# One attention stage for latent and grouped attention, one-hot expert rows, early preparation of the second block

## The reference

```python
p = h @ w_in
cq, ckv, kr = p[..., :o0], p[..., o0:o1], p[..., o1:o2]
gq, gk, gv = p[..., o2:o3], p[..., o3:o4], p[..., o4:]
qa = (rmsnorm(cq, q_norm) @ w_q_up)    # latent attention
kva = (rmsnorm(ckv, kv_norm) @ w_kv_up)
qb = rmsnorm(gq per head, gq_norm)     # grouped attention, 2 key heads
x = x + g1 * (concat(oa, ob) @ w_out)
```

## Time and profile before

| | us |
|---|---|
| median of 3 runs (lowest, highest) | 3480.21 (3478.96, 3483.86) |
| profiled execution, its time | 3482.5 |
| profiled execution, its span | 3480.7 |
| first block ends, second block's first projection starts | 1564.1, 1607.6 |
| layer 0's output projection starts | 1928.05 |
| layer 0's experts start, layer 1's | 2036.9, 2938.3 |

### The profile page before, as it was taken

The page is one execution under the profiler, slowest core; times in us unless marked ns, Lnnn a source line. Parts: engine busy times, 40 slices in busy tenths (PEclk is TensorE's granted clock), DMA queues, the critical chain, the costliest instruction groups (busy, mean ns, idle before and its releaser), DMA issues. The chain is left out here.

```text
span 3480.7 us, 31524 instructions
## 1 busy us (share of the span) xinstructions
PE 2873.4 (83%) x12630; PEld 1621.3 (47%) x12630; DVE 1009.5 (29%) x2513; ACT 571.0 (16%) x1269; POOL 239.2 (7%) x408
## 2 busy tenths in 40 slices
PE   6799989998799999995788868788838986877874
PEld 3476646854476547843456432232214463322221
DVE  2443423413443514402155321111123153111112
ACT  1222401101223301102223110000000141000000
POOL 0000004000000000000000000110011020011001
PEclk9999999999999999997898879899968987989997
DMA  5245445534155434533300359999974213999996
GB/s 205 74 162 207 146 145 170 194 136 145 50 192 202 150 139 162 177 115 73 109 25 25 117 211 427 428 427 427 426 305 118 73 43 125 428 427 427 428 427 243
DMA packets 188683, 740.54 MB, mean 213 GB/s; under 512 B 16400, under 2 KB 25600, under 8 KB 163440
## 3 DMA queue, kind: packets, MB, share of 16 engines
q1 hardware_dynamic: 163600, 667.51, 49.1%
q0 software_dynamic: 24928, 70.90, 6.2%
HBM read 711.52 MB, written 28.67 MB: 213 GB/s over the span
## 5 line engine op out<-in xcount | busy, mean ns | idle before, releaser
L2063 PE MATMUL bank<-wslot,xgT 128*64 128x512 f32 x1040 | 541.0, 681 | 187.5 <-DMA wslot<-in_moe_w_up 94.1
L2064 PE MATMUL bank<-wslot,xgT 128*64 128x512 f32 x1040 | 542.3, 682 | 0.0
L458 PE MATMUL bank<-h1T,wslot 128*128 128x256 f32 x2176 | 482.8, 385 | 3.0 <-DVE fpad L1464 3.0
L458 PEld LDWEIGHTS bank<-h1T,wslot 128*128 128x128 f32 x2176 | 417.8, 193 | 62.9 <-issue 6.5
L2063 PEld LDWEIGHTS bank<-wslot,xgT 128*64 128x64 f32 x1040 | 156.5, 156 | 512.1 <-issue 512.1
L2080 DVE TENSOR_TENSOR hid<-gs,bank 64x512 f32<-64x512 f32 x65 | 67.9, 1045 | 696.9 <-ACT gs L2074 696.9
L2118 PE MATMUL bank<-wslot,aT 128*64 128x512 f32 x1040 | 230.6, 595 | 2.8 <-DVE aT L532 1.5
L435 PE MATMUL bank<-wslot,hT 128*128 128x512 f32 (+3 forms) x576 | 224.7, 553 | 5.1 <-issue 4.3
L435 PEld LDWEIGHTS bank<-wslot,hT 128*128 128x128 f32 x576 | 113.3, 198 | 111.9 <-issue 99.3
L2064 PEld LDWEIGHTS bank<-wslot,xgT 128*64 128x64 f32 x1040 | 156.5, 156 | 8.7 <-issue 8.7
L435 PE MATMUL bank<-wslot,actT 128*128 128x512 f32 x352 | 151.5, 593 | 5.6 <-DVE actT L1503 5.6
(11 more groups left out here) (342 smaller groups left out, 3196.3 us busy)
## 6 DMA issues: line engine op xcount, KB each, us to landing
wslot<-in_moe_w_gate SPq DMA_DIRECT2D x65, 2048.0 KB, 17.2
wslot<-in_moe_w_up SPq DMA_DIRECT2D x65, 2048.0 KB, 12.8
wslot<-in_moe_w_down SPq DMA_DIRECT2D x65, 2048.0 KB, 15.8
wslot<-in_w_in SPq DMA_DIRECT2D x36, 2048.0 KB, 9.0
wslot<-in_w_ada SPq DMA_DIRECT2D x24, 2048.0 KB, 8.1
wslot<-in_ffn_w_up SPq DMA_DIRECT2D x20, 2048.0 KB, 8.7
y_rows<-yo POOLq DMA_DIRECT2D x130, 128.0 KB, 7.1
wslot<-in_w_proj_ssd SPq DMA_DIRECT2D x8, 2048.0 KB, 7.8
```

Source lines behind the costliest of these rows:

```text
L458: ins = pe.matmul(b.t[:, 0:width], w[:, k, j * P:(j + 1) * P], xT(k), start=(k == 0), stop=(k == kc - 1))
L2063: pe.matmul(bk.t[other, :], xt.t[:, k, mine], wg[:, k, :], start=(k == 0), stop=(k == KD - 1))
L2064: ins = pe.matmul(bk.t[mine, :], xt.t[:, k, mine], wu[:, k, :], start=(k == 0), stop=(k == KD - 1))
```

## The change

- `joint_attention` takes the place of both attention functions. Its four projections from `hT` come first (`cq`, `ckv`, `gq`, `gkv`), then `qup` and `kvup`, all by `tokens_later`, and the plan's order follows. Then one pipeline of 64 jobs runs, context tiles first. Grouped queries are kept two heads to a tile (`qbT`), and the keys (`kbT`) are kept twice with the other half blanked, where before the queries were. `kaT` lies in `hT`'s memory.
- `Second` holds the second block's tensors from the start of the kernel. Its `beside` puts the modulation columns and the norms and transposes of the context tiles into `K.rest` during `first_ffn` of layer 1. Its `begin` scales and norms the latent tiles, and `ready(t)` writes a tile into `hT` just ahead of its `cq` matmuls.
- The gate row is fetched during the projections (`fetch_gate`), in both layers. `noted` records marks where `settle` stood after the attentions. `add_gated` waits tile by tile.
- Expert rows: `route` writes the normed rows into `hT`'s memory (`h_rows`) and stores nothing to `h_dram`. `select` builds for each pair a matrix of 0 and 1 per token tile on VectorE, and `turn_rows` multiplies the rows by it: 8 x 4 matmuls a pair in layer 0, 8 x 2 in layer 1. `gather`, `tokidx` and the steps that made it are gone.
- The first block's `acc`, `gate` and two `decay` buffers lie in the second block's tensors.

The diff, cut to its core:

```diff
...
+    def noted(self):
+
+        self.settled = [(s, s.count) for s in (self.pe, self.dve, self.act) if s.count]
...
+    def tokens_later(self, key, xT, n_tiles, deps, use, each=None):
...
+            ready = each(t) if each else ()
             bank = self.banks.next()
 
             @self.block.tensor
             def _(pe):
-                for due in self.due(pe, landed, *deps, *bank.free):
+                for due in self.due(pe, landed, *deps, *ready, *bank.free):
...
+        K.tokens_later(("cq",), xT, NT2, [], use_low(QL, "q_norm", cqT), hready)
+        K.tokens_later(("ckv",), xT, NT2, [], use_low(KVL, "kv_norm", ckvT), hready)
+        K.tokens_later(("gq",), xT, NT2, [], use_gq, hready)
+        K.tokens_later(("gkv",), xT, NT2, [], use_gkv, hready)
+        fetch_gate((K.pe, K.pe.count))
...
+            def use_q(t, bank, mk, n=n):
                 b = tok.next()
...
+            K.tokens_later(("qup", n), lambda k, t: cqT[:, k, t * P:(t + 1) * P], NT2, low, use_q)
...
+            K.tokens_later(("kvup", n), lambda k, t: ckvT[:, k, t * P:(t + 1) * P], NT2, low, use_kv)
+        projected = (K.pe, K.pe.count)
...
+        grouped_jobs(0)
+        grouped_jobs(1)
+        latent_jobs(0)
+        latent_jobs(1)
+        for t in range(2, NT2):
+            grouped_jobs(t)
+            latent_jobs(t)
         pipeline(jobs, 7)
-        K.settle()
...
+    def select(i):
         if i >= len(pairs):
             return
-        x, q = xg.next(), pairs[i][0] // 2
-
-        @block.gpsimd
-        def _(g):
-            sig = K.moved.next()
-            for due in K.due(g, (sig, sig.count) if sig.count else None, *routed, *x.free):
-                g.wait_ge(*due)
-            got[i] = (x, sig.mark(g.indirect_dma_start(
-                x.t[:, :], None, h_dram, bass.IndirectOffsetOnAxis(ap=tokidx[:, q:q + 1], axis=0)).then_inc(sig.sem, 16), 16))
+        a, f, s, q = away.next(), first.next(), sel.next(), pairs[i][0] // 2
+
+        @block.vector
+        def _(v):
+            for due in K.due(v, *slotted, *s.free):
+                v.wait_ge(*due)
+            m = K.dve.mark(v.tensor_scalar(a.t[:, :], slot[:, :], float(-PAIR * q), None, ALU.add).then_inc(K.dve.sem, 1))
+            for due in K.due(v, m):
+                v.wait_ge(*due)
+            for t in range(tiles):
+                m = K.dve.mark(v.tensor_scalar(f.t[:, t, :], K.c("iota"), a.t[:, 2 * t:2 * t + 1], None, ALU.is_equal)
+                               .then_inc(K.dve.sem, 1))
+            for due in K.due(v, m):
+                v.wait_ge(*due)
+            for t in range(tiles):
+                K.mv = K.dve.mark(v.scalar_tensor_tensor(out=s.t[:, t, :], in0=K.c("iota"), scalar=a.t[:, 2 * t + 1:2 * t + 2],
+                                                         in1=f.t[:, t, :], op0=ALU.is_equal, op1=ALU.add)
+                                  .then_inc(K.dve.sem, 1))
+        got[i] = (s, K.mv)
 
     def turn_rows(i):
...
-                    ins = pe.transpose(bk.t[:, j * P + pr.start:j * P + pr.stop], x.t[pr, kk * P:(kk + 1) * P],
-                                       K.ident[pr, pr])
+                    for t in range(tiles):
+                        ins = pe.matmul(bk.t[:, j * P:(j + 1) * P], h_rows[t][:, kk * P:(kk + 1) * P], s.t[:, t, :],
+                                        start=(t == 0), stop=(t == tiles - 1))
...
-    gather(0)
-    gather(1)
+    select(0)
     turn_rows(0)
+    select(1)
     for i in range(len(pairs)):
-        gather(i + 2)
         if i:
             turn_hidden(i - 1)
         widen(i)
         turn_rows(i + 1)
+        select(i + 2)
...
+        self.h_rows = [flat[:, D * t:D * (t + 1)] for t in range(self.tiles)]
...
-            step(v.tensor_scalar(qsu[:, 0, :], self.yrow[:, :], 7, None, ALU.logical_shift_right))
-            step(v.tensor_scalar(qsu[:, 1, :], self.yrow[:, :], PAIR - 1, None, ALU.bitwise_and))
-            step(v.tensor_copy(qsf[:, :, :], qsu[:, :, :]))
-            step(v.tensor_tensor(spot[:, :, :], bc(iota(PAIR).unsqueeze(1), TK, PAIR), bc(qsf[:, 1, :].unsqueeze(2), TK, PAIR),
-                                 ALU.is_equal))
-            step(v.tensor_tensor(pair[:, :, :], bc(iota(npair).unsqueeze(1), TK, npair),
-                                 bc(qsf[:, 0, :].unsqueeze(2), TK, npair), ALU.is_equal))
-            K.mv = step(v.tensor_tensor(ident[:, :, :, :], pair[:, :, :].rearrange("p (t k) n -> p t k n", k=2),
-                                        bc(K.c("token")[:, 0:T].unsqueeze(2).unsqueeze(2), T, 2, npair), ALU.mult))
-        placed = K.mv
-        b2 = K.banks.next()
-
-        @K.block.tensor
-        def _(pe):
-            for due in K.due(pe, placed, *b2.free):
-                pe.wait_ge(*due)
-            for i in range(TK):
-                ins = pe.matmul(b2.t[:, 0:npair], spot[:, i, :], ident[:, i // 2, i % 2, :], start=(i == 0), stop=(i == TK - 1))
-            K.mp = K.pe.mark(ins.then_inc(K.pe.sem, 1))
+            K.mt = step(v.tensor_copy(self.slot[:, :], self.yrow[:, :]))
         late, dif, ex, den = F("late", [T, 4]), F("dif", [T]), F("ex", [T, 4]), F("den", [T])
...
+        quiet = lambda: None
+        K.rest += [quiet, lambda: modulated(0), lambda: modulated(1), lambda: norm(0), lambda: norm(1), quiet, quiet,
+                   lambda: turn(0), quiet, lambda: turn(1)]
...
+            st, inv, m = K.inverse_rms((w["junk"], w["stat"]), x[:, t, :], D, *K.settled)
+
+            @K.block.vector
+            def _(v):
+                for due in K.due(v, m, rm):
+                    v.wait_ge(*due)
+                marks[t] = K.dve.mark(v.scalar_tensor_tensor(out=x[:, t, :], in0=x[:, t, :], scalar=inv, in1=row[:, :],
+                                                             op0=ALU.mult, op1=ALU.mult).then_inc(K.dve.sem, 1))
+            st.free = [marks[t]]
...
+        for t in range(TT):
+            b = xn.next()
+            self.normed[2 + t] = b, K.norm_rows(w, x[:, t, :], b.t[:, :], D, marks[t], *b.free)
...
+        if t not in self.hdeps:
+            b, m = self.normed[t]
+            self.hdeps[t] = turn_into_hT(self.K, b, t, self.hT, lambda k, t: gain[:, 0, k:k + 1],
+                                         lambda k, t: shift[:, 0, k:k + 1], m, deps)
+        return self.hdeps[t]
...
+                            for s, row in enumerate(g1):
+                                gm.append(K.move(g, row, modrows[l, MG1, s].partition_broadcast(P), read))
...
```

More of the change, by code:

```diff
@@ L1451, in first_ffn @@
                            [(K.dve, K.dve.count)])
+        if second:
+            second.beside(w)
         done = []
@@ L1570, in first_block @@
                 spread_bias(K)
[L1571 removed]
+            first_ffn(K, l, x, hT, cols, silu_c, modrows, second if l else None)
             deps = [(K.dve, K.dve.count)]
@@ new lines, in joint_attention @@
+        projected = (K.pe, K.pe.count)
+        K.flush()
+        early.close()
+        w["prob"] = K.turn(ctx, "prob", 4, [P, 512])
+        w["probT"] = K.turn(ctx, "probT", 3, [P, 512])
+        w["turns"], w["share"] = 0, 2
+        orow = K.turn(ctx, "orow", 2, [P, 4 * VA])
+        for b in w["prob"].bufs:
+            b.free = [projected]
+        for b in w["probT"].bufs + orow.bufs:
+            b.free = [(K.pe, K.pe.count), (K.act, K.act.count), (K.dve, K.dve.count)]
+        done = {t: [] for t in range(NT2)}
@@ L1880, in grouped_attention @@
         pipeline(jobs, 7)
-        K.settle()
+        K.noted()
+    return done
 SPAN_R = 2 * (SEQ // GRID_W) - 1
```

443 lines of the change are left out of this document (232 added, 211 removed).

## The result

The changed kernel takes 3355.7 us (median of 4 runs, 3348.5 to 3357.2) against 3479.7 us for the kernel before in the same rounds. The ratio is 0.9637, 95% interval 0.962 to 0.9654: 3.6% faster. The forecast was 3322 us with a range of 3298 to 3375. The time lies in the range, 34 us above the forecast.

What follows compares the result with a forecast made beforehand. Transfers were taken to bound the expert stages, TensorE and its waits the rest. Savings of 107.8 + 10.7 + 8.8 + 30.7 = 158.0 us from 3482.5 gave 3324.5, or 3322 us on the median's footing; range 3298 to 3375.

Steps and rivals of the forecast that it cites:

- Part 1: Joint attention stage, first block's last matmul to output projection: 252.5 us, 111.4 saved, 107.8 net of costs before it.
- the latent tiles 2 and 3: Start of the projections: their norms and hT writes end after two cq tiles, leaving 9 us uncovered for both.
- A sign that came true: Projections: the prediction is wrong if transposes wait for VectorE by more than 20 us in all.
- A: Layer 0's experts become bound by TensorE: 32.4 us a pair at clock 0.90, 27 us lost, 3349 us; chance 0.13.
- C: Expert streams: transfers gain nothing from dropped gathers, as slots hold weights back; 30.7 us lost, 3352 us; chance 0.08.
- Rival B: Projections: the tiles' chains still show, half the gain of 101 us is lost, 3372 us; chance 0.13.
- The FFN's share: Layer 1's first_ffn: the moved context preparation costs 18 transposes, 2 us, plus 1 us of gaps.
- Part 2: Output projections, both layers: early gates and noted marks remove waits for g and the low clock; 10.7 us saved.
- Part 3: Starts of the expert stages: selection replaces gathers and the first tile escapes the low clock; 8.8 us saved together.
- Part 4: Expert streams: without gathers a pair's transfers take 30.7 us, not 31.9, and stay the bound; 30.7 us saved in all.
- D: Expert selection: records cost far more than 0.111 us; at 0.40 the kernel takes 3663 us; chance 0.01.
- E: Expert selection: weight loads aren't hidden behind matmuls, 0.22 us a record, 3420 us; chance 0.04.

Runs made afterwards that it cites:

- Experiments 1 and 2: Changed kernel with the zero fill of y_rows issued behind the norm_final_w row (3334.6 us), or behind the gate rows in both layers (3332.4 us).
- experiment 7: Changed kernel with the zero fill behind the gate rows, kbT blanked before the final norm, and hT tile 3's transposes right after tile 2's: 3325.5 us.
- experiment 5: Changed kernel with each of the eight projections run over its four tiles at once, chains and transposes behind: 3421.4 us.
- experiment 6: Context preparation moved from the first block's last FFN to between the blocks: changed kernel 3361.5 us; version with late fill and reordered chains 3338.6 us.
- experiment 9: Both kernels timed and profiled again, unedited: changed kernel 3351.0 us, kernel before 3488.0 us in its one execution.
- The run with TensorE waiting: Changed kernel with gate rows fetched after the attention, full settle, and output-projection matmuls waiting for the gate rows too: 3368.3 us.
- late-gate run: Changed kernel with gate rows fetched only after the attention and a full settle in both layers; only VectorE waits for the gate: 3354.8 us.
- Experiment 8: Changed kernel with gate rows fetched after the attention and full settle: 3354.8 us; with the output-projection matmuls waiting for them as well: 3368.3 us.
- experiment 3: Changed kernel with every selection product made twice into the same bank: 3449.5 us.
- late-fill run: Changed kernel with the zero fill of y_rows issued behind the fetch of the gate rows in both layers: 3332.4 us.
- second run of experiment 6: Version with late zero fill and reordered chains (3325.5 us), with the context's preparation run between the blocks: 3338.6 us.

## Why the prediction was right, and where it was off

- **Part 1, the stage.** Forecast 252.5 us, 269.0 and 272.5 in the two profiles. The step that failed is the term "the latent tiles 2 and 3, whose norms and hT writes end after `cq` tiles 0 and 1 ... are through, 9 us for both". It counts the engines' steps and has no term for the landing of the row of `norm_final_w`. The sentence on moves ("three more moves on POOL's queue ... behind nothing that TensorE needs soon") looks only at moves that the change adds. It passes over one that the change shifts: the line that makes `Experts`, and in it the zero fill, now stands ahead of the final norm. The waits are 19.72 + 1.97 + 2.68 = 24.4 us in the changed kernel and 2.93 + 1.98 + 2.69 = 7.6 us with the fill late. Experiments 1 and 2 give the price: 16 to 23 us by the medians, 14 to 17 in the stage against the second profile. Shown.
- **A sign that came true.** The prediction called itself wrong "if transposes in the projections wait for VectorE by more than 20 us in all". They wait 19.72 + 2.82 + 0.59 + 2.11 + 0.27 = 25.5 us in the changed kernel. Also the projections took 156 us at a clock of 0.91, for about 140 above 0.95. That the time still fell into the range is owed to the range's width, which was drawn for rivals A to C and not for this cause. The 34 us above the forecast are made of the stage's 16.5 to 20, the 5 us of the first block in most executions, layer 0's 3.5, and the rest below what these runs tell apart.
- **The other terms of part 1** held. The last `gq` and `gkv` chains wait 2.82, 0.59 and 2.11 us (4.5 forecast). With the fill late the stage takes 255.2 us, and 245.2 with the orders of experiment 7, for 252.5. Rival B (the chains still show) is refuted, and experiment 5 shows that the 51 us of idle time and the clock of 0.82 come with the tiles at once. Jobs: 111.6 us for 112.5.
- **The FFN's share** was a little low: 4.4 us shorter without the preparation (experiment 6), for 3.0 forecast; against the second profile of the kernel before (253.4 us from `mergedT` to `actT`) it is 2.8. The other 5 us of the first block are scatter (experiment 9).
- **Part 2.** The size was about right: 10.7 us forecast and 6.87 counted in part 1 make 17.6. The run with TensorE waiting has 6.98 + 5.16 us of waits and 2.86 + 2.59 of slower matmuls, 17.6 too, less 0.78 + 1.39 that the late-gate run waits anyway; the medians differ by 13.5. The prediction's 2.8 us a layer for the low clock is 1.6 us in layer 0 of the kernel before (64 records in 29.28 us, at the high clock 27.70) and 2.8 in layer 1 (16.67 for 13.90). It put the gain down to "gates fetched early". Experiment 8 shows that with the wait on VectorE the early fetch adds nothing; whether it would have been enough by itself was not run.
- **Part 3** held: −4.2 us for −4.4 in layer 0 and −6.9 for −7.8 in layer 1. Both rows of the table also hold part 2's 2.8 us for the output projection.
- **Part 4** held within its noise: 31.8 us for 33.0 over both streams, the gather 1.1 us a pair for 1.23. Layer 0 gave 3.5 us less than forecast. Between VectorE's last copy of expert output and the read of the gate row lie 17.4 us instead of 13.3, which is as much. Why was not tried.
- **Rivals A, C, D, E** are refuted: TensorE waits 1.7 us a pair at clock 1.00 (A), the pair takes 30.8 us (C), a record costs 0.111 us where it counts (D, E; experiment 3). On the rule behind E: the Trainium skill ("TensorE: Matmul & The Clock Gate", Part 3, The mechanism) says that a load overlaps with matmuls in flight only when the row group differs, though the same section also names loads into a background weight buffer. By the rule without that exception 64 more records would be 14 us more work a pair. TensorE's work went from 377.85 / 13 = 29.1 us a pair to 35.9, so by 6.8; the trace does not agree with it.
- **The 7 us** between the profile and the median are scatter of single executions; the second profile of the changed kernel took 3355.3 us, and the median of that round was 3351.0. With the fill late the median is 3332.4, 10 us from the forecast: the stage's 2.7, the FFN's 1.4, layer 0's 3.5, and the rest below what these runs tell apart.

## What to carry to other kernels

Before costing a moved line, list every instruction that it issues, constructors included, and for each queue ask both what stands ahead of it now and what now stands behind it. A large transfer that nobody waits for belongs behind every small one that somebody waits for. When a change removes a wait by two edits at once, when the data comes and who waits for it, try each alone; here one of them was enough. Profile both kernels more than once before you explain a difference of 5 us: the first profile of the changed kernel flattered one stretch by 3.5 us, and that of the kernel before a whole block by 5. And waits of 2 to 3 us in close order can cost more than their sum: the granted clock was lower with them, and taking 4.3 us of them out gave 6.9 by the medians and 10.1 in the stage.

## What the hardware showed that I had not expected

- The zero fill of 3.6 MB out of SBUF keeps the DMA share at 0.91 with only 207 GB/s (window 1578 to 1597 of the changed kernel) and takes 19.7 to 20.3 us, more than twice what its bytes would need at the weights' 427 GB/s (8.6 us).
- TensorE's granted clock was 0.83 in 39 us that held 34.3 us of matmul and two waits of 2 and 2.7 us behind one of 3.1; it was 1.00 in 40 us with 38.2 us of matmul and one wait of 1.85. The two figures came again, 0.82 in the late-fill run and 1.00 in the second run of experiment 6. With a wait of 19.7 to 20.0 us in front, the next 33 us had 0.89 in the changed kernel's first profile and 0.79 in its second, with the same small waits in both.
- In the expert stage the clock went from 0.90 to 1.00 when TensorE's share of busy time went from 81% to 94%, by filling its gaps with work of no use for the speed of the transfers.
